# Streaming encoder block on one core: half-size loads of the last weight blocks, and a rearranged final normalization

## The reference

```python
for _ in range(DEPTH):                                  # DEPTH = 1
    h = rms_norm(x, norm_in_w)                          # x is (1, 512, 2048)
    proj = jnp.einsum('bsd,dc->bsc', h, w_in)
    ...
    out_a = swa_sink_attention(qa, ka, va, sinks_a) * jax.nn.silu(a_g)
    ...
    out_b = mla_attention(qb_nope, qb_rope, kb_nope, kb_rope, vb) * jax.nn.silu(b_g)
    mixed = jnp.concatenate([out_a, out_b], axis=-1)
    x = x + jnp.einsum('bsc,cd->bsd', mixed, w_out)     # w_out is (2048, 2048)
return rms_norm(x, final_norm_w)
```

## Time and profile before

| | |
|---|---|
| median of 3 runs | 665.0 us (664.98 to 665.48) |
| the profiled execution's own time | 665.19 us |
| its span, first to last instruction | 663.4 us |
| PE busy | 653.5 us, 99% of the span |
| DVE, ACT, POOL busy | 66%, 50%, 41% |
| mean granted TensorE clock | 0.995 |

### The profile page before, as it was taken

How to read it: one execution, slowest core, us unless ns; L and a number is a source line. 1 busy time by engine, 2 the same in 40 slices (tenths; PEclk the granted TensorE clock), 3 DMA queues, 4 the chain that set the end, 5 groups by cost and what they waited for, 6 DMA issues and landing times.

```text
span 663.4 us, 8807 instructions
## 1 busy us (share of the span) xinstructions
PE 653.5 (99%) x3126; PEld 548.2 (83%) x3126; DVE 437.9 (66%) x706; ACT 332.4 (50%) x625; POOL 273.3 (41%) x133
## 2 busy tenths in 40 slices
PE   9999999999999999999999999999999999999994
PEld 8888888888888888888888888988888888887883
DVE  6868132889694554564554566787652749989996
ACT  6833231311334664664663657767864443554545
POOL 0044443354344424424424416766778566030012
PEclk9999999999999999999999999999999999999998
DMA  8732333133213223123122313122022841487526
GB/s 300 278 121 87 105 99 100 66 125 96 95 66 121 69 81 111 64 77 114 65 95 96 98 62 127 52 78 74 24 87 74 327 162 54 172 306 255 205 104 254
DMA packets 21944, 81.96 MB, mean 124 GB/s; under 512 B 2448, under 2 KB 2704, under 8 KB 19856
## 3 DMA queue, kind: packets, MB, share of 16 engines
q1 hardware_dynamic: 18000, 72.88, 31.8%
q10 hardware_dynamic: 3904, 8.54, 3.8%
HBM read 77.22 MB, written 4.19 MB: 123 GB/s over the span
## 4 chain that ended last, share of the span: by engine, by line
PE 98%; DVE 1%; ACT 0%; issue 0%; ACTq 0%; DVEq 0%
PE bank L1424 29%; PE bank L1427 29%; PE bank L1428 29%; PE bank L1689 1%; PE bank L1568 1%; PE bank L1578 1%; PE bank L1675 1%; PE bank L1676 1%; PE bank L1454 1%; PE bank L1591 1%; PE bank L1590 1%; PE bank L1447 1%; PE bank L1444 1%; PE bank L1492 0%; PE bank L1487 0%; PE bank L1480 0%
## 5 line engine op out<-in xcount | busy, mean ns | idle before, releaser
L343 POOL TENSOR_TENSOR w_lo<-w_raw,w_hi 128x1024 fp32r<-128x1024 f32 x84 | 206.0, 2459 | 269.4 <-ACT w_hi L449 269.3
L1424 PE MATMUL bank<-x_hi,w_hi 128*128 128x512 f32 x496 | 193.7, 391 | 0.0
L1427 PE MATMUL bank<-x_hi,w_lo 128*128 128x512 f32 x496 | 193.3, 390 | 0.0
L1428 PE MATMUL bank<-x_lo,w_hi 128*128 128x512 f32 x496 | 193.2, 390 | 0.0
L449 ACT ACTIVATE w_hi<-w_raw 128x1024 fp32r<-128x1024 f32 x93 | 98.1, 1055 | 130.8 <-PE bank L1424 112.4
L1428 PEld LDWEIGHTS bank<-x_lo,w_hi 128*128 128x128 f32 x496 | 93.1, 188 | 19.8
L1424 PEld LDWEIGHTS bank<-x_hi,w_hi 128*128 128x128 f32 x496 | 93.2, 188 | 18.7 <-DVE mixed L1101 0.2
L1427 PEld LDWEIGHTS bank<-x_hi,w_lo 128*128 128x128 f32 x496 | 93.2, 188 | 18.0
L1424 PE MATMUL bank<-w_hi,mx_hi 128*128 128x512 f32 x128 | 50.3, 393 | 0.0
L1428 PE MATMUL bank<-w_lo,mx_hi 128*128 128x512 f32 x128 | 49.9, 390 | 0.0
L1427 PE MATMUL bank<-w_hi,mx_lo 128*128 128x512 f32 x128 | 49.9, 390 | 0.0
(11 more groups left out here) (245 smaller groups left out, 1236.3 us busy)
## 6 DMA issues: line engine op xcount, KB each, us to landing
w_raw<-w_stream SPq DMA_DIRECT2D x93, 512.0 KB, 3.3
t_raw<-w_pairs SPq DMA_DIRECT2D x15, 1024.0 KB, 4.8
y<-x_nat ACTq DMA_DIRECT2D x4, 1024.0 KB, 6.3
out<-y SPq DMA_DIRECT2D x6, 512.0 KB, 3.2
xs<-x_t SPq DMA_DIRECT2D x4, 512.0 KB, 5.2
mixed<-x_t SPq DMA_DIRECT2D x4, 512.0 KB, 5.1
t_raw<-w_pairs ACTq DMA_DIRECT2D x1, 1024.0 KB, 7.7
fw<-final_w ACTq DMA_DIRECT2D x4, 256.0 KB, 4.8
```

Of the source, the lines that this page charges most:

```text
L343: pool.tensor_tensor(w_lo[:, s % HL, :], w_raw[:, s % RAW, :], w_hi[:, s % HL, :].bitcast(F32), ALU.subtract)\
L1424: ins = pe.matmul(dst, ah, bh, start=start, stop=False, skip_group_check=goes_on)
L1427: pe.matmul(dst, al, bh, start=False, stop=False, skip_group_check=goes_on)
L1428: return pe.matmul(dst, ah, bl, start=False, stop=stop, skip_group_check=goes_on)
```

## The change

1. The loads of visits 4 to 15 are cut in two of 512 KB. The first half (slots 0 and 1) is issued when the first products of the visit four earlier are done, the second at that visit's end as before. The readers wait for both halves.
2. PE's order at the end of q = 0: M1 and M6 of visit 15 now stand ahead of M7 of visit 14.
3. ACT's two squares move from visit 10 to visit 12, and the table load to visit 13.
4. Tail: ACT scales one block of tiles 1 and 0 instead of two (and one more of tile 1). POOL scales blocks 1 and 2 of tile 1, and later block 2 of tile 3 instead of block 1. DVE takes block 1 of tile 0 and block 1 of tile 3, and its work on tile 0 stands earlier. Tile 1 leaves in three stores instead of two.

```diff
             for v in range(4, VISITS):
-                if v == 11:
-                    sp.wait_ge(m_done, 6)
-                else:
-                    sp.wait_ge(t_used, 2 * v - 6 if v < 11 else 2 * v - 8)
-                sp.dma_start(t_raw[v % 4][:, :, :], w_pairs[v, :, :, :]).then_inc(t_landed[v % 4], 16)
-            for t in TILES_DONE[:3]:
+                for g in range(2):
+                    if v == 11:
+                        sp.wait_ge(m_done, 6 if g else 2)
+                    else:
+                        sp.wait_ge(t_used, (2 * v - 7 if v < 11 else 2 * v - 9) + g)
+                    two = slice(2 * g, 2 * g + 2)
+                    sp.dma_start(t_raw[v % 4][:, two, :], w_pairs[v, :, two, :]).then_inc(t_landed[v % 4], 16)
+            sp.wait_ge(left[1], 1)
+            sp.dma_start(out[0, P:2 * P, 0:SEQ], y[:, 1, 0:SEQ]).then_inc(stored, 16)
+            sp.wait_ge(middle[1], 1)
+            sp.dma_start(out[0, P:2 * P, SEQ:CE], y[:, 1, SEQ:CE]).then_inc(stored, 16)
+            sp.wait_ge(middle[1], 2)
+            sp.wait_ge(right[1], 1)
+            sp.dma_start(out[0, P:2 * P, CE:], y[:, 1, CE:]).then_inc(stored, 16)
+            for t in TILES_DONE[1:3]:
...
-            pool.wait_ge(o_squared, 13)
-            gained(0, 3)
...
+            scale(0, 1, 1, 8, middle)
+            scale(0, 1, 2, 9, middle)
+            pool.wait_ge(o_squared, 13)
+            gained(0, 3)
+            scale(1, 0, 3, 11, right)
             pool.wait_ge(y_added, 18)
-            scale(1, 0, 3, 11, right)
-            pool.wait_ge(y_added, 19)
-            scale(2, 3, 1, 8, left)
+            scale(2, 3, 2, 10, right)
...
-                if v == 10:
+                if v == 12:
                     for q in range(2):
                         act.wait_ge(y_added, 7 + q)
                         square(2 * q + 1, 2, 8 + q)
+                if v == 13:
                     act.activation(preloaded[:, :], eps[:, :], ACT.Sqrt)
...
-            scale(0, 1, 2)
-            act.wait_ge(o_gained, 9)
-            act.activation(y[:, 1, 2 * SEQ:3 * SEQ], y[:, 1, 2 * SEQ:3 * SEQ], ACT.Copy, scale=fin[:, 1, 2:3]).then_inc(right[1], 1)
+            scale(0, 1, 1)
...
-            scale(1, 0, 2)
+            scale(1, 0, 1)
...
             reciprocal(0, 1)
-            scale_gain(0, 1, 3)
             add(0, 2, 2, 9, 11, op=ALU.subtract)
             add(0, 2, 0, 10, 13, op=ALU.subtract)
+            scale_gain(0, 1, 3)
+            rest(3, 0, 13)
             add(2, 2, 5, 11)
+            reciprocal(1, 0)
+            scale(1, 0, 1, 8)
             add(3, 3, 5, 11, 4)
-            rest(3, 0, 13)
             add(3, 3, 7, 12, 16)
-            reciprocal(1, 0)
             scale_gain(1, 0, 2)
             add(2, 3, 3, 13, 6)
+            reciprocal(2, 3)
+            scale(2, 3, 1, 8)
             add(2, 2, 3, 13, 15, op=ALU.subtract)
-            reciprocal(2, 3)
             add(2, 2, 1, 14, 19, op=ALU.subtract)
+            rest(4, 2, 16)
             scale_gain(2, 3, 3)
-            rest(4, 2, 16)
-            scale(2, 3, 2, 10)
             reciprocal(3, 2)
...
                 last_of_pair(m6(v, 0), v)
-                if v == 15:
-                    last_of_pair(m5(v, 0), v)
-                last_of_pair(m7(v, 0), v)
+                if v == 13:
+                    m7(v, 0)
+            m7(14, 0)
+            last_of_pair(m5(15, 0), 15)
+            last_of_pair(m7(15, 0), 15)
```

More of the change, by code:

```diff
@@ L292, in build @@
         left, right = ([sem(f"{side}{t}") for t in range(TOK)] for side in ("left", "right"))
+        middle = {1: sem("middle1")}
         block = ctx.enter_context(nc.Block())
@@ L335, in _ @@
                 sp.dma_start(out[0, 2 * P:3 * P, SEQ * c:SEQ * c + SEQ], y[:, 2, SEQ * c:SEQ * c + SEQ]).then_inc(stored, 16)
-            sp.wait_ge(stored, 16 * 10)
+            sp.wait_ge(stored, 16 * 11)
         @block.gpsimd
@@ L725, in part_high @@
                 if g == 0 and v < 8:
-                    act.wait_ge(t_landed[v % 4], 16 * (v // 4) + 16)
+                    act.wait_ge(t_landed[v % 4], 32 * (v // 4) + 16)
                 else:
@@ L1273, in part_sums @@
                 raw = t_raw[v % 4]
-                dve.wait_ge(t_landed[v % 4], 16 * (v // 4) + 16)
+                dve.wait_ge(t_landed[v % 4], 32 * (v // 4) + 16)
                 if v < 8:
@@ L1388, in scale @@
                 ys = y[:, t, SEQ * c:SEQ * c + SEQ]
-                dve.tensor_scalar(ys, ys, fin[:, t, 2:3], None, ALU.mult).then_inc(right[t], 1)
+                dve.tensor_scalar(ys, ys, fin[:, t, 2:3], None, ALU.mult).then_inc(left[t], 1)
             dve.wait_ge(fws_landed, 32)
```

## The result

| | before | after |
|---|---|---|
| median of 19 runs each | 665.24 us (664.77 to 666.00) | 666.24 us (665.42 to 667.97) |
| ratio of the times, after to before | | 1.0016, 95% interval 1.0010 to 1.0022 |
| profiled execution, its span | 665.19, 663.4 us | 665.84, 663.9 us |

The change makes the kernel slower by 1.0 us, 0.16%: resolved by 19 runs, and less than the 0.2% that the prediction counts as a difference. 663.4 was forecast, with 664.7 as the range's upper end: the forecast gain of 1.6 us did not come.

What follows compares the result with a forecast made beforehand. PE, busy 653.5 of 663.4 us, was taken as the bound, with the stores' volume setting the end. 0.88 from PE's gaps plus 0.72 from earlier stores made 1.6: 665.0 - 1.6 = 663.4 us, range 662.7 to 664.7.

Steps and rivals of the forecast that it cites:

- Loads in halves land 1.5 us sooner, and DVE gains 1.2 us: Visits 4 and 8: parts complete 1.5 us sooner, DVE's load waits go (1.2 us), PE ends 0.88 us sooner.
- Rival B: PE's gaps mostly stay, half loads landing no sooner; about 0.5 us from stores alone: 664.5; 12 in 100.
- The added issues cost nothing: On SP: the extra load issues cost nothing, as SP has 4 us between loads.
- Squares: ACT's move removes DVE's 0.61 us wait at visit 11; with the loads, DVE's last split ends at 642.4.
- M1 and M6 earlier: PE, visit 15: they start 0.68 us sooner, M6 at 642.8; without the other edits PE waits 0.5 us.
- Rival D: DVE's splits come late after all, M6 of visit 15 waits up to 0.5 us: 663.9; 8 in 100.
- Nearly no slack on DVE's tail: DVE's tail starts at 642.4 and reaches the last addition at 653.9; PE leaves that bank at 653.87.
- POOL's scales, 0 for tile 3's: Tail: DVE begins its tile 3 scale ahead of POOL, hold 0; bound 0.5 us if POOL comes first.
- Stores leave earlier, 0.72 us net: Tail: tile 3's right half issued at 655.6 instead of 656.84; stores add 0.72 us to PE's 0.88.
- rival A: Tail: DVE late at the last addition or POOL holding a store loses 0.5 to 1.0 us: 664.2; 25 in 100.
- C: Tail: POOL and DVE hold one another, 1.1 us per full meeting; three give 666.7; 5 in 100.
- the prediction's own signs of being wrong: DVE's additions late without a PE wait, DVE scales above 1 us, or store data ending at 661 or later.

Runs made afterwards that it cites:

- e7: The kernel before with loads of visits 4 to 15 in halves, each half contiguous in HBM, same issue times as e1; 665.69 against 665.13 us, ratio 1.0008.
- e1: The kernel before with only the loads of visits 4 to 15 in two halves of rows; 666.40 against 665.12 us, ratio 1.0014.
- e11: The changed kernel with whole loads and PE's old order; 666.03 against 665.47 us for the kernel before, ratio 1.0011.
- e6: The changed kernel with whole loads, POOL's scale of tile 3 waiting for the last addition; 665.49 against 665.13 us for the kernel before, ratio 1.0004.
- e4: The kernel before with only the tail's edits; 666.17 against 665.12 us, ratio 1.0010.
- e10: The kernel before with squares moved, PE's new order, another tail and e7's contiguous half loads; 664.34 against 665.47 us, ratio 0.9983.

## Why the prediction was wrong

- *Loads in halves land 1.5 us sooner, and DVE gains 1.2 us*: **the step that failed.** It priced a half by a 512 KB load of other weights (3.3 us). A half lands after 5.0 us, at visit 4 after 6.8 where the whole took 6.1; DVE's additions start 0.44 us later, and PE's gaps are 1.48 us where 0 was forecast: 1.48 us of the miss. Rival B had the place (halves land no sooner), but no loss, and its reason, halves that share the engines, holds for e7 too, which lost nothing in the gaps. e1 beside e7 shows what made the loss: halves of rows, issued early, land later than the same halves in one piece. By what mechanism stays open.
- *The added issues cost nothing*: on SP, yes. Some 0.2 us (0.13 to 0.27 in the profiled executions) appear outside the span with every kernel that has them.
- *Squares*: 0.61 us of waiting removed, as forecast (34.18 to 33.56). But DVE's last split ended at 644.04 and not at 642.4. The difference, 1.64, is the 1.2 that the loads didn't give and the 0.44 that they took.
- *M1 and M6 earlier*: "by itself, 0.5 us of waiting". Beside the moved squares it was 0.11 (the edit by itself was not run), with 0.65 us less lateness in return (e11). Rival D's place was right, its price a fifth.
- *Nearly no slack on DVE's tail*: there was none, and the wrong side of it was met. From the first tail addition to the last the count gave 10.91 us; it took 12.09, since the holds (0.61 and 0.70) were not all absorbed and the root and the reciprocal of tile 3 cost 0.20 and 0.27 of waits. DVE also began 1.47 us later than counted, and PE's end was 1.40 later: 1.18 + 1.47 - 1.40 = 1.25 late.
- *POOL's scales, 0 for tile 3's*: the bound of 0.5 was the case, at 0.70. The doubt that the Trainium skill raises (GPSIMD Engine Reference, section 1, Specifications: shared SBUF interfaces, contention for a 2-port mode or two SBUF inputs) is borne out for the plain scale too: 1.19 us beside POOL, 0.49 with POOL away in e6. Whether it ran in such a mode, no run shows. With that, the forecast's sum would have had 0.7 us less gain.
- *Stores leave earlier, 0.72 us net*: they do (8.59 to 7.33 behind the last addition), but the right half waited for an addition 1.25 us late, so nothing was left. This is rival A's mechanism, with C's meeting of POOL and DVE as its cause; the sum of A was 0.5 to 1.0 us lost and it was 1.25.

Of the prediction's own signs of being wrong all three came: the last addition late with no wait for PE ahead of it, scales on DVE above 1 us, and the DMA engines still full from 661.5 to 662.4 (403 GB/s).

Together: 1.48 for the gaps and 0.72 for the tail (0.72 expected, nothing found) are 2.2 of the 2.8 us between 663.4 and 666.24. Of the rest, 0.24 is that the median before is now 665.24, and some 0.2 lies outside the span.

## What to carry to other kernels

Price a smaller load by one that is issued into the same traffic and read with the same pattern, not by its size: here half the bytes took 4.4 to 5.0 us and the whole 4.8, and where the engines were full, halves of rows completed the part 0.7 us later than the whole. Where two bounds of a tail have the same height, find both before moving work: here late additions and the volume of stores each gave 9.0 us, and only the order that lowered both was faster. On VectorE, which gates the last chain, let only operations that read a bank run beside GpSimd's work, and keep GpSimd's scales out of the stretch in which VectorE scales.

## What the runs showed of the hardware

- Plain scales (`TENSOR_SCALAR`, one SBUF input, 128 x 512) are held beside a GpSimd operation that began first: 1.19 us in the changed kernel, 1.18 in e4, 0.49 without it. A `scale_gain` took 1.35 and 1.50 instead of 0.74. Additions from a bank aren't: two in 1.48 us beside POOL's scales at 647.37, and two in 1.48 with POOL idle in e6 at 654.85. One plain scale, at 650.91, took 0.49 while POOL's `gained` was still shown as busy to 651.1; why it got through is open.
- Loads of 4 KB out of each 8 KB row, issued early, completed visit 4's part 6.7 to 6.8 us after the second issue; the same halves in one piece took 6.0 (6.2 in e10), the whole 5.9 to 6.3. From 583 to 586 the first moved 335 GB/s (DMA share 0.93), halves in one piece 411, whole rows 393.
- Twelve more load instructions went with some 0.2 us more between the span and the execution's own time, in each of five kernels: 1.92 to 2.20 us in every execution, against 1.73 to 1.86 with whole loads.
